# A streaming-encoder layer with a routed expert stage: output product, second norm and router in token tiles, slot arithmetic on GpSimd, and running sums later in the first stage

## The reference

```python
h = rms_norm(x, norm_mix); proj = h @ w_in
o_a = forgetting_attention(...)      # needs cumsum(log_sigmoid(ff + fox_f_bias))
o_b = gla_chunked(...)               # needs cumsum of log_a inside chunks of 64
o_c = mamba2_branch(...)             # needs cumsum(dt * a) inside chunks
x = x + sum_b(sigmoid(gate_b) * (o_b @ w_branch[b])) @ w_out
t = rms_norm(x, norm_ffn)
g_w, g_sel = top_k(softmax(t @ w_router_grp + b), 1)       # 4 groups
e_in = (t @ w_router_exp + b)[the 4 experts of group g_sel]
top_w, top_i = top_k(softmax(e_in), 2)                     # 2 of them
out = sum_e combine[:, e] * (silu(t @ w_gate[e]) * (t @ w_up[e])) @ w_down[e]   # 16 experts
x = x + out
```

## Time and profile before

| | |
|---|---|
| Median of 3 runs (lowest, highest) | 893.75 us (892.7, 897.91) |
| Profiled execution: time, span | 893.08 us, 891.3 us |
| PE busy, PEld busy | 842.3 us (95%), 673.0 us (76%) |
| DVE, ACT, POOL busy | 576.7, 474.3, 82.0 us |
| Chain that ended last | PE 61%, DMA 25%, DVE 6%, ACT 4% |
| DMA | 164.23 MB, mean 184 GB/s |

### The profile page before, as it was taken

How to read it: one execution, slowest core, us unless ns; L and a number is a source line. 1 busy time by engine, 2 the same in 40 slices (tenths; PEclk the granted TensorE clock), 3 DMA queues, 4 the chain that set the end, 5 groups by cost and what they waited for, 6 DMA issues and landing times.

```text
span 891.3 us, 11385 instructions
## 1 busy us (share of the span) xinstructions
PE 842.3 (95%) x4144; PEld 673.0 (76%) x4144; DVE 576.7 (65%) x645; ACT 474.3 (53%) x552; POOL 82.0 (9%) x106
## 2 busy tenths in 40 slices
PE   3989999999999899999999999499999999999994
PEld 3767777777877678888888888188888888887783
DVE  5456436766745897324334424779888988898893
ACT  5464535454455242322232323447788878887782
POOL 5310000000000110100000000003112111211001
PEclk9999999999999999999999999789999999999998
DMA  7321112212112021332223465249999999999993
GB/s 227 124 96 47 48 48 95 75 69 95 49 48 95 0 95 50 129 106 95 94 95 146 184 220 232 118 156 396 378 386 369 361 372 383 379 362 369 379 353 48
DMA packets 60172, 164.23 MB, mean 184 GB/s; under 512 B 9593, under 2 KB 10706, under 8 KB 60131
## 3 DMA queue, kind: packets, MB, share of 16 engines
q1 hardware_dynamic: 51504, 145.89, 43.9%
q0 software_dynamic: 4464, 12.66, 6.2%
q10 hardware_dynamic: 4162, 5.13, 1.6%
HBM read 154.16 MB, written 13.11 MB: 188 GB/s over the span
## 4 chain that ended last, share of the span: by engine, by line
PE 61%; DMA 25%; DVE 6%; ACT 4%; issue 2%; SPq 0%; POOL 0%; ACTq 0%; POOLq 0%; DVEq 0%
PE bank L1830 17%; PE bank L1832 16%; PE bank L1831 16%; DMA mstage<-in_w_exp_gate 9%; DMA mstage<-in_w_exp_up 8%; DMA mstage<-in_w_exp_down 7%; PE bank L1946 1%; PE bank L1977 1%; PE bank L1962 1%; ACT whi L691 1%; DMA xin<-in_x 1%; PE bank L1934 1%; PE bank L2078 1%; DVE wlo L704 1%; PE bank L2183 1%
## 5 line engine op out<-in xcount | busy, mean ns | idle before, releaser
L704 DVE TENSOR_TENSOR wlo<-mstage,whi 128x2048 fp32r<-128x2048 f32 x96 | 218.1, 2290 | 31.6 <-ACT whi L691 31.5
L691 ACT ACTIVATE whi<-mstage 128x2048 fp32r<-128x2048 f32 x96 | 183.5, 1919 | 41.6 <-PE bank L1832 35.8
L704 DVE TENSOR_TENSOR wlo<-stage,whi 128x2048 fp32r<-128x2048 f32 (+1 forms) x40 | 89.6, 2239 | 107.3 <-ACT whi L691 106.7
L1830 PE MATMUL bank<-hTh,whi 128*128 128x512 f32 x368 | 149.0, 405 | 0.0
L1832 PE MATMUL bank<-hTh,wlo 128*128 128x512 f32 x368 | 143.6, 390 | 0.0
L1831 PE MATMUL bank<-hTl,whi 128*128 128x512 f32 x368 | 143.3, 390 | 0.0
L691 ACT ACTIVATE whi<-stage 128x2048 fp32r<-128x2048 f32 (+1 forms) x40 | 75.0, 1874 | 78.8 <-PE bank L1832 76.1
L1830 PE MATMUL bank<-whi,xTh 128*128 128x512 f32 (+1 forms) x264 | 104.6, 396 | 1.7 <-DVE wlo L704 1.7
L1832 PE MATMUL bank<-whi,xTl 128*128 128x512 f32 (+1 forms) x264 | 101.6, 385 | 0.0
L1831 PE MATMUL bank<-wlo,xTh 128*128 128x512 f32 (+1 forms) x264 | 101.1, 383 | 0.0
L1830 PEld LDWEIGHTS bank<-hTh,whi 128*128 128x128 f32 x368 | 69.1, 188 | 16.1 <-issue 2.6
(11 more groups left out here) (384 smaller groups left out, 1316.6 us busy)
## 6 DMA issues: line engine op xcount, KB each, us to landing
mstage<-in_w_exp_gate SPq DMA_DIRECT2D x32, 1024.0 KB, 12.7
mstage<-in_w_exp_up SPq DMA_DIRECT2D x32, 1024.0 KB, 12.4
mstage<-in_w_exp_down SPq DMA_DIRECT2D x32, 1024.0 KB, 12.4
stage<-in_w_in SPq DMA_DIRECT2D x28, 1024.0 KB, 5.0
stage<-in_w_branch SPq DMA_DIRECT2D x6, 1024.0 KB, 5.1
stage<-in_w_out SPq DMA_DIRECT2D x4, 1024.0 KB, 5.0
xin<-in_x SPq DMA_DIRECT2D x4, 512.0 KB, 5.6
x<-in_x SPq DMA_DIRECT2D x4, 512.0 KB, 7.0
```

Source lines behind the costliest of these rows:

```text
L691: nc.scalar.activation(whi[:, s, :, 0:n], source_of(u)[:, :, 0:n], ACT.Copy).then_inc(hi_ready, 1)
L704: nc.vector.tensor_tensor(wlo[:, s, :, 0:n], source_of(u)[:, :, 0:n], whi[:, s, :, 0:n].bitcast(F32), ALU.subtract).then_inc(lo_ready, 1)
L1830: t.matmul(out, lhs[0], rhs[0], start=start, stop=False)
```

## The change

The running sums: the copies into `cumhl` and their differences become an item of their own ("cumh"), behind the last piece of the first block instead of inside "logs"; "bcum" goes from the second block's second half to the third block's first.

The output product goes by token tile: tile 0 with all four units, then for tiles 1 to 3 one half at a time, and between the halves the turning of the tile before, its logits (now 128 tokens by 20 columns) and its counts. The third unit gets a buffer of its own (`whi4`), split earlier; the fourth goes to the slot of the last gate unit. Squares, root, norm, split and choice are made per tile, 18 VectorE instructions for each choice, the root in three GpSimd instructions per tile. The permutation goes by tile; that of tile 3 is one float32 product per chunk, unsplit. Rows lie in chunk order, so that x1's columns are reordered by the norm. The slot arithmetic goes from VectorE to GpSimd: after a copy of the counts by ScalarE (`pl`), 28 instructions in series up to `place_done`, for which `hotitem` waits. Bits and shifts are replaced by comparisons, the scan by four shifted additions. VectorE splits unit `U_MOE + 1` before the permuted rows. The core of the diff:

```diff
--- before.py
+++ after.py
     early = {(0, 0, 1): [("small",)], (0, 0, 2): [("lo", 2)], (0, 0, 3): [("loga",)], (0, 1, 1): [("logs",)],
-             (1, 0, 3): [("tokrows",)], (1, 1, 0): [("bcum",)]}
+             (0, 1, 3): [("cumh",)], (1, 0, 3): [("tokrows",)], (2, 0, 1): [("bcum",)]}
...
+    for i in range(NT):
+        for nh in range(2):
+            uses[2 * (i % 2) + nh].append(("out", i, nh))
+        uses[4].append(("h2T", i))
+        uses[5].append(("h2T", i))
+        uses[6].append(("lg", i))
+        uses[7].append(("pos", i))
...
+        def out_halves(i):
+            return (0, 1) if i == 0 else (1, 0)
+        def out_bank(i, nh):
+            return 2 * (i % 2) + nh
...
+            elif u == U_OUT + 2:
+                act.wait_ge(full[3], turn(3, ("gate", 5)) + 1)
+            elif u == U_OUT + 3:
+                wait_unit(act, U_OUT - 1)
...
-                    sp.wait_ge(full[7], turn(7, "perm") + 1)
-                elif k == 10:
-                    sp.wait_ge(full[0], turn(0, "logitsT") + 1)
+                    sp.wait_ge(full[3], turn(3, "perm") + 1)
+                    sp.wait_ge(acc_in[NT - 1], 16)
+                    sp.wait_ge(h2_out[NT - 1], 16)
...
-            pool.wait_ge(x1_sq, NT)
-            step(g.tensor_scalar(ssq[:, :], ssq[:, :], 1.0 / D, EPS, ALU.mult, ALU.add))
-            step(g.tensor_tensor(rst[:, :], ssq[:, :], mhalf[:, 0:NT], ALU.pow), r2_done, 1)
+            for q in range(3):
+                step(g.memset(pad24[q][:, :], 0.0))
+            for i in range(NT):
+                one, two = out_halves(i)
+                pool.wait_ge(x1_sq, 2 * i + 1)
+                step(g.tensor_scalar(ssq[:, i:i + 1], msq[:, i, one:one + 1], 1.0, EPS, ALU.mult, ALU.add))
+                pool.wait_ge(x1_sq, 2 * i + 2)
+                step(g.tensor_tensor(ssq[:, i:i + 1], ssq[:, i:i + 1], msq[:, i, two:two + 1], ALU.add))
+                step(g.tensor_tensor(rst[:, i:i + 1], ssq[:, i:i + 1], mhalf[:, 0:1], ALU.pow), r2_done, i + 1)
+            pool.wait_ge(r_ab, NT)
...
+            for k, oh in enumerate((oh1, oh2)):
+                step(g.tensor_tensor(a12[:, k, :, :].rearrange("p i (g e) -> p i g e", e=EPG),
+                                     oh[:, :, :].unsqueeze(2).to_broadcast([P, NT, NEG, EPG]), group_of, ALU.mult))
+            pool.wait_ge(pl_done, 1)
+            total = pl[:, 64:80]
+            place = pl[:, 0:64].rearrange("p (i e) -> p i e", e=16)
+            extra = pad24[0][:, 8:24]
+            step(g.tensor_scalar(extra, total, 128.0, None, ALU.is_gt))
+            for lim in (256.0, 384.0):
+                step(g.tensor_scalar(t16[:, :], total, lim, None, ALU.is_gt))
+                step(g.tensor_tensor(extra, extra, t16[:, :], ALU.add))
+            for q, shift in enumerate((1, 2, 4, 8)):
+                fro = pad24[(0, 1, 2, 1)[q]]
+                to = incl[:, :] if q == 3 else pad24[(1, 2, 1)[q]][:, 8:24]
+                step(g.tensor_tensor(to, fro[:, 8:24], fro[:, 8 - shift:24 - shift], ALU.add))
+            step(g.tensor_tensor(diff[:, :], incl[:, :], extra, ALU.subtract))
+            step(g.tensor_tensor(diff[:, :], diff[:, :], ecst[:, :], ALU.add))
...
+            for k in range(2):
+                step(g.tensor_tensor(pik[:, k, :, :, :], pi16[:, :, :, :],
+                                     a12[:, k, :, :].unsqueeze(1).to_broadcast([P, 2, NT, 16]), ALU.mult))
...
+            step(g.tensor_tensor(vals[:, :, :, 0:1], tokid[:, :].unsqueeze(1).to_broadcast([P, 2, NT]).unsqueeze(3),
+                                 pf[:, :, 0, :].unsqueeze(3), ALU.subtract), place_done, 1)
...
+            split_hi(act, U_OUT + 2)
             for k in range(4, KD):
                 act.wait_ge(y_added, k + 1)
                 y_hi(k)
...
+            split_hi(act, U_OUT + 3)
...
+            squares(0, 0)
+            squares(0, 1)
+            for i in range(1, NT):
+                if i > 1:
+                    squares(i - 1, 1)
+                if i == NT - 1:
+                    split_hi(act, U_MOE)
+                for nh in range(2):
+                    turned_rows(i - 1, nh)
+                rows_hi(i - 1)
+                squares(i, 0)
+            turned_rows(NT - 1, 1)
+            split_hi(act, U_MOE + 1)
+            squares(NT - 1, 1)
+            turned_rows(NT - 1, 0)
+            act.wait_ge(r2_done, NT)
+            act.wait_ge(xs_done, 2)
+            step(a.activation(xn2[:, NT - 1, :], xn2[:, NT - 1, :], ACT.Copy, scale=rst[:, NT - 1:NT]), xn2_done, NT)
+            act.dma_start(h2d[(NT - 1) * P:NT * P, :], xn2[:, NT - 1, :]).then_inc(h2_out[NT - 1], 16)
+            split_hi(act, U_MOE + 2)
+            act.wait_ge(r_arg, 1)
+            step(a.activation(g4[:, :, :], g4[:, :, :], ACT.Exp))
+            step(a.activation(ex2[:, :], ex2[:, :], ACT.Exp), r_exp, 1)
+            act.wait_ge(free[7], turn(7, ("pos", NT - 1)) + 1)
+            step(a.activation(pl[:, :], bank[7][:, 0:80], ACT.Copy), pl_done, 1)
...
+                    if g == 5 and s == 0:
+                        split_lo(dve, U_OUT + 2)
...
+            def normed(i):
+                dve.wait_ge(r2_done, i + 1)
+                dve.wait_ge(gainb_in, 16)
...
+            def choose(i):
+                n = turn(6, ("lg", i)) + 1
+                if i == 0:
+                    dve.wait_ge(route_consts, 1)
+                    dve.wait_ge(pad_out, 16)
+                dve.wait_ge(r2_done, i + 1)
+                dve.wait_ge(full[6], n)
+                step(v.scalar_tensor_tensor(out=lg[:, i, :], in0=bank[6][:, 32 * i:32 * i + 20], scalar=rst[:, i:i + 1],
+                                            in1=rbias[:, :], op0=ALU.mult, op1=ALU.add), free[6], n)
...
+                step(v.tensor_tensor(grouped(ab[:, i, :]), oh12[:, :].unsqueeze(1).to_broadcast([P, NEG, EPG]), group,
+                                     ALU.mult), r_ab, i + 1)
+            def hot_rows(i):
+                n = turn(7, ("pos", i)) + 1
+                dve.wait_ge(full[7], n)
+                step(v.scalar_tensor_tensor(out=key2[:, i, :], in0=ab[:, i, 0:2], scalar=-1024.0,
+                                            in1=bank[7][:, 16 * i:16 * i + 2], op0=ALU.mult, op1=ALU.add), free[7], n)
+                step(v.tensor_tensor(hot2[:, i, :, :] if i < NT - 1 else hot3[:, :, :],
...
+                                     key2[:, i, :].unsqueeze(2).to_broadcast([P, 2, P]), ALU.is_equal), hot2_done, i + 1)
...
+            add_rows(0, 0)
+            add_rows(0, 1)
+            for i in range(1, NT):
+                if i > 1:
+                    add_rows(i - 1, 1)
+                    hot_rows(i - 2)
+                normed(i - 1)
+                if i < NT - 1:
+                    choose(i - 1)
+                    rows_lo(i - 1)
+                    add_rows(i, 0)
+            split_lo(dve, U_MOE)
+            add_rows(NT - 1, 0)
+            choose(NT - 2)
+            gained(1)
+            add_rows(NT - 1, 1)
+            gained(0)
+            hot_rows(NT - 2)
+            rows_lo(NT - 2)
+            choose(NT - 1)
+            hot_rows(NT - 1)
+            split_lo(dve, U_MOE + 1)
+            for q in range(4):
+                perm_lo(q)
+            dve.wait_ge(r_exp, 1)
...
             split_lo(dve, U_MOE + 2)
+            dve.wait_ge(place_done, 1)
+            for k in range(2):
+                step(v.tensor_tensor(hotitem[:, 4 * k:4 * k + 4, :], iotai[:, :].unsqueeze(1).to_broadcast([P, 4, ITEMW]),
+                                     pf[:, k, 1, :].unsqueeze(2).to_broadcast([P, 4, ITEMW]), ALU.is_equal))
...
+            def out_product(i, nh, kh):
+                b = out_bank(i, nh)
+                u = U_OUT + 2 * kh + nh
+                c = slice(i * P, (i + 1) * P)
+                if i == 0:
                     pe.wait_ge(y_done, 4 * kh + 4)
                     pe.wait_ge(lo_ready, u + 1)
...
+                if kh == 0:
+                    take(b, ("out", i, nh))
+                for j in range(4):
+                    ins = passes(whole(b), (yTh[kh][:, j, c], yTl[kh][:, j, c]), (whi_of(u)[:, j, :], wlo_of(u)[:, j, :]),
+                                 kh == 0 and j == 0, kh == 1 and j == 3)
+                if kh == 1:
+                    ins.then_inc(full[b], 1)
+                elif i == NT - 1:
+                    ins.then_inc(unit_used, 1)
...
+            def permute(i, half):
+                pe.wait_ge(hot2_done, i + 1)
+                if i == NT - 1:
+                    pe.wait_ge(xn2_done, NT)
+                else:
+                    pe.wait_ge(xnh_done, i + 1)
+                    pe.wait_ge(xnl_done, i + 1)
+                for c in range(4 * half, 4 * half + 4):
+                    b = c // 2
+                    if i == 0 and c % 2 == 0:
+                        take(b, "perm")
+                    out = bank[b][:, 256 * (c % 2):256 * (c % 2) + 256]
+                    cc = slice(c * P, (c + 1) * P)
                     if i == NT - 1:
```

(56 more changed lines are left out.)

406 lines of the change are left out of this document (162 added, 244 removed).

## The result

| | kernel before | changed kernel |
|---|---|---|
| median of the timed runs, us | 894.89 (892.7 to 897.91) | 882.88 (881.31 to 883.63) |
| profiled execution, us (span) | 893.08 (891.3) | 883.63 (881.8) |
| mean TensorE clock in it | 0.984 | 0.988 |

The account below looks back on a forecast made before the run. TensorE was taken as the bound, with DMA second in the experts' stage. The sum was 893.08 - 2.9 (first stage) - 3.2 (up to the experts) - 2.0 (late experts) = 885.0 us; forecast 885.5, range 876.5 to 894.

Parts of the forecast that it names:

- First stage: Running sums moved later: TensorE's waits for ScalarE's squares go, 2.9 us gained, bounds 0 and 3.5.
- Tile 0's fourth unit: Output product, tile 0: the fourth weight unit's split comes late on ScalarE, 1.9 us charged (0 to 4).
- Tiles with router work: Transposes, logit products and counts of three tiles inside the output product add 8.4 us on TensorE.
- Up to the first expert product: Output product, router and permutation end earlier: first expert product at 578.5 instead of 591.5 us, 13.0 us gained.
- VectorE as the bound: Rival: the tile loop is bound by VectorE, choice instructions cost 0.30 us or evictions are late; 888 to 890, chance 0.14.
- GpSimd's chain: Slot table: 28 dependent instructions, 10.2 us plus waits for VectorE, delay the fourth expert unit; 3.2 of 13.0 us remain gained.
- The rival without any shutting out: Rival: VectorE doesn't block GpSimd, so the slot table's chain ends at 585.4; total 878 us, chance 0.22 (chain hidden).
- The long chain: Rival: each GpSimd instruction of the slot table costs 0.9 us, making the kernel slower at 902 us; chance 0.12.
- Clock at the fourth unit: After TensorE idles for the slot table, half clock makes the fourth expert unit take 2.72 + 2.1 = 4.8 us.
- Late experts: Held-back weight loads start earlier, so two slow items late in the experts go: 2.0 us gained (0 to 2.2).
- Signs named in advance: Trace signs of a right forecast: earlier first expert product, TensorE idle before the fourth unit, stretched GpSimd instructions, no late DMA wait.

Follow-up runs that it names:

- the rest alone: The changed kernel with the running sums back in their old places, column halves, tiles and router as changed: 887.63 us, ratio 0.9911 to the kernel before.

## Why the prediction was right, step by step

The order of events was right: a gain from the sums, a large one from the tiles, most of it turned into a wait for GpSimd's table with half clock behind it, and a small one from earlier weights. The sizes were less good.

- **First stage** (2.9, bounds 0 to 3.5). The long wait is gone and the third too; of the 3.5 us of waits 0.5 are left. By distances inside the traces it gave 3.4 us at the output product, shortest against shortest, so the mechanism was right. In the profiled pair only 2.2 of it is visible, because half clock near 300 us held on longer in that execution. By the timed runs it is 4.3 (2.6 to 6.1), more likely than not above my upper bound: I priced the waits, not the half clock that can follow them (last section).
- **Tile 0's fourth unit** (1.9): 2.09, of which 1.55 come from the DMA issues, as the run that moved them shows.
- **Tiles with router work** (8.4): eight logit products show as 1.85 us for 16 rows of both halves, 1.65 by start to next; transposes 1.0. The permutation of tiles 0 to 2 begins at 564.07, 55.1 us after the product's start; I had 54.2.
- **Up to the first expert product** (67.1 after the start): 68.4. Of the 1.3 us, 0.8 stand at the choice of tile 3 (59.5 against 58.7), 0.3 in the choice itself (4.0 us for 18 instructions, 0.22 each against 0.205), and 0.2 in the counts and the last permutation. This step of the forecast, 13.0 gained, was 1.2 too large; no single error.
- **VectorE as the bound** (rival, 888 to 890): no wait of TensorE for an eviction stands between 505 and 573. The rival falls.
- **GpSimd's chain**: own time 10.4 us against 10.2, instructions of 0.20 to 0.49 us with 0.07 to 0.09 between. The shutting out cost 3.9 us where I had 5.6: I had charged two splits at 2.8 and 2.3 and 0.5 for others, but a split costs GpSimd its length less the instruction that it holds, 1.9 each, and no other VectorE instruction in that stretch shows in GpSimd's times. First to fourth unit: 16.15 us against 17.5. The rival without any shutting out (878) falls. The long chain (902) falls too; its own sum was off, since 28 instructions of 0.9 us put the fourth unit at 611.0, not 613.4. In the forecast 596.0 and 4.8 make 600.8, where I wrote 600.6.
- **Clock at the fourth unit** (4.8 us): 4.40 here, 4.33 to 5.29 in the other profiles of this order. The run with extra products shows that the idle time was its cause.
- **Late experts** (2.0, bounds 0 to 2.2): 3.1, above my bound. The mechanism, lead of the weights, is shown. The term was too small because 0.7 us come from shorter items (of it 0.5 from the transposes' stride, which I had seen in the diff and priced at nothing), and the other 2.4 from the long items, of which there were two full ones and the start of a third, not two.
- **Signs named in advance.** First expert product earlier by 12 to 14 us without the first stage, 15 to 17 with it: 11.85 and 14.1, just short of both. TensorE idle 7 to 10 us before the fourth unit: from the end of the third unit to it are 7.8 us, but 2.1 of them are the table's products, so 5.7 are idle. GpSimd's instructions stretched to 2.2 us, one wait of 2.1 us in the product stage, no long item late: as said.

The errors are small and of both signs: -0.7, -1.2, +1.8, +1.1, and 0.3 behind the last mark. The total, 885.5 forecast and 882.88 measured, owes some of its nearness to that, which is luck. The gain itself, 8.1 us forecast against 12.0 by the medians, is a third too small. Part of that is the first stage (4.3 us). The rest goes along with the clock, though no run shows how much of it: its mean is 0.988 to 0.990 in the timed executions of the changed kernel and 0.980 to 0.986 in those of the kernel before, and my sum has a price for half clock at one place only.

## What to carry to other kernels

When a serial stage is broken up, follow the smallest thing that it delivered (here a table of 46 numbers) to its consumer: it is late next, and on an in-order engine whatever stands behind its wait is late too. A dependent chain on GpSimd is priced by its own instructions, plus the length, less one held instruction, of every VectorE instruction beside it that has two SBUF inputs or is a copy from SBUF to SBUF. Where TensorE must idle some us in front of dense work, products that compute nothing may keep its clock up (1.25 and 1.5 us here, in the traces). Where loads bound the end of a stage, as here with 282 to 283 us from their release, an earlier release is a gain of its own.

## What I had not expected of the hardware

- A copy with one SBUF input on VectorE (0.99 us for 1536 columns) shuts GpSimd out as a two-input subtraction does: held by one copy, a 64-column instruction of 0.32 us takes 1.00.
- Half clock lasts differently long after the same wait. Near 300 us TensorE waits 3.03 to 3.08 us in every version, and in all thirteen profiles the granted clock falls to 0.50 there. Summed over the windows from 300 to 316 us, 1.7 us of clock are missing in nine of them and 3.4 in four (time multiplied by one less the granted clock). The way from there to the output product is 203.5 us in the nine and 204.6 to 205.2 in the four.
- Behind the wait of 2.7 us near 55 us the granted clock stays at 1.00 in the kernel before, and the next two products take 1.10 us. In the run of the rest alone (its row stands with that run) it falls to 0.50 from 56 to 58 us, they take 2.05, and 1.7 us of clock are missing. So the same wait costs its length in one execution and up to 1.7 us more in another, and a single profile is no better than that.

The row of the kernel before:

```profile
54.59 1.10 PE L1934 MATMUL bank<-qsq,blk 128*128 128x512 f32 x2 [2.67 <-ACT qsq L1046]
```
